# Two routing stages: x split in halves, the modulation behind the logits, fewer filler matmuls, an earlier table load

## The reference, cut to what matters

```python
for l in range(DEPTH):                       # DEPTH = 2
    mod = (silu(c) @ ada_w[l] + ada_b[l]).reshape(bsz, 6, 1, D_MODEL)
    sh1, sc1, g1, sh2, sc2, g2 = (mod[:, i] for i in range(6))
    h = rms_norm(x, norm1_g[l]) * (1.0 + sc1) + sh1
    x = x + g1 * mixer(h)                    # even layer: gating + differential attention; odd: dilated attention + conv
    h = rms_norm(x, norm2_g[l]) * (1.0 + sc2) + sh2
    x = x + g2 * grouped_moe(h, router_w, router_b, moe_w_gu[l], moe_w_down[l])

def grouped_moe(h, ...):
    probs = softmax(t @ router_w)            # 16 experts
    sel = (probs + router_b).reshape(-1, 4, 4)
    grp = argmax(sum of the top 2 of each group); experts = the top 2 in that group
    gates = p_top / sum(p_top)
    act = silu(g) * u * gate_dense           # g, u: h @ w_gu[e], 1024 x 1024 an expert
    y = einsum('etf,efd->td', act, w_down)   # 512 x 1024 an expert
```

## Time and profile before

| | |
|---|---|
| median of 3 runs | 871.66 us (870.56, 871.66, 875.34) |
| the profiled execution | 875.81 us |
| its span, first to last instruction | 874.0 us |
| PE / DVE / ACT / POOL busy | 90% / 43% / 20% / 2% of the span |
| PEld busy | 47% |
| mean granted clock of TensorE | 0.976 of 2.4 GHz |
| DMA | 294 MB, mean 336 GB/s |

### The profile page before, as it was taken

One profiled execution on the slowest core, in us unless ns is written; L12 is line 12 of the kernel. 1 busy time (PEld: TensorE's weight loads), 2 busy tenths in 40 slices (PEclk: granted clock), 3 DMA queues, 4 the chain that ended last, 5 costly groups with the idle time before them and its releaser, 6 DMA issues.

```text
span 874.0 us, 12136 instructions
## 1 busy us (share of the span) xinstructions
PE 789.9 (90%) x4984; PEld 412.6 (47%) x4984; DVE 375.0 (43%) x892; ACT 174.9 (20%) x413; POOL 14.5 (2%) x61
## 2 busy tenths in 40 slices
PE   4999999999999998778999999898999999898864
PEld 2566454454343333224858778764454333333221
DVE  1188862573322230205699765354563312221203
ACT  2041321511111110103000423451511111110101
POOL 2000010000000000000000000000000000000000
PEclk9999999999999999979999999999989999999978
DMA  9999998797899999999999225204977899999993
GB/s 348 389 386 387 387 387 322 298 374 277 328 427 425 426 424 427 427 421 390 385 386 357 97 97 193 98 1 145 428 272 285 333 430 423 428 423 428 427 421 150
DMA packets 65115, 294.05 MB, mean 336 GB/s; under 512 B 2721, under 2 KB 3361, under 8 KB 49185
## 3 DMA queue, kind: packets, MB, share of 16 engines
q1 hardware_dynamic: 64352, 290.62, 83.8%
q10 hardware_dynamic: 560, 2.10, 0.6%
q0 software_dynamic: 144, 0.52, 0.2%
HBM read 292.18 MB, written 1.05 MB: 336 GB/s over the span
## 4 chain that ended last, share of the span: by engine, by line
PE 52%; issue 24%; DMA 12%; DVE 6%; ACT 4%; POOL 0%; DVEq 0%; SPq 0%; POOLq 0%; ACTq 0%
PE bank L856 16%; PE bank L852 11%; PE bank L1103 8%; DMA ring<-w_gu_dram 7%; DMA ring<-w_down_dram 5%; PE bank L1125 4%; PE bank L1089 3%; PE bank L737 2%; PE bank L697 1%; PE bank L1140 1%; PE bank L761 1%; ACT tail L1314 1%; PE bank L752 1%; PE bank L714 1%; PE bank L923 1%
## 5 line engine op out<-in xcount | busy, mean ns | idle before, releaser
L1103 PE MATMUL bank<-ring,scr 128*64 128x512 f32 (+1 forms) x1024 | 197.0, 629 | 34.6 <-DMA ring<-w_gu_dram 22.2
L856 PE MATMUL bank<-hT,ring 128*128 128x256 f32 x640 | 142.3, 381 | 0.4 <-DVE hT L1668 0.4
L1103 PEld LDWEIGHTS bank<-ring,scr 128*64 128x64 f32 (+1 forms) x1024 | 56.3, 132 | 162.7 <-issue 131.8
L856 PEld LDWEIGHTS bank<-hT,ring 128*128 128x128 f32 x640 | 120.5, 190 | 17.8 <-issue 1.6
L1125 PE MATMUL bank<-ring,scr 128*64 128x512 f32 (+1 forms) x544 | 106.0, 625 | 5.4 <-DMA ring<-w_down_dram 5.0
L1598 DVE SCALAR_TENSOR_TENSOR gb<-ring,small,gb 128x512 f32<-128x512 f32 x84 | 63.1, 752 | 2.9
L1125 PEld LDWEIGHTS bank<-ring,scr 128*64 128x64 f32 (+1 forms) x544 | 30.6, 131 | 62.4 <-issue 60.5
L852 PE MATMUL bank<-ring,xh 128*128 128x512 f32 x128 | 56.9, 598 | 0.7 <-ACT xh L1314 0.7
L852 PE MATMUL bank<-ring,hT 128*128 128x512 f32 x128 | 56.4, 596 | 0.6 <-ACT hT L1348 0.5
L2105 DVE SCALAR_TENSOR_TENSOR hT<-bank,small,gb 128x512 f32<-128x512 f32 x26 | 19.5, 751 | 84.1 <-PE bank L1125 82.6
L1859 DVE SCALAR_TENSOR_TENSOR tail<-scr,col,tail 128x256 f32<-128x256 f32 x120 | 47.9, 474 | 0.0
(11 more groups left out here) (266 smaller groups left out, 761.3 us busy)
## 6 DMA issues: line engine op xcount, KB each, us to landing
ring<-w_gu_dram SPq DMA_DIRECT2D x60, 2048.0 KB, 20.4
ring<-w_down_dram SPq DMA_DIRECT2D x28, 2048.0 KB, 17.9
ring<-ada_w_dram SPq DMA_DIRECT2D x24, 2048.0 KB, 15.8
ring<-od_w_in_dram SPq DMA_DIRECT2D x9, 2048.0 KB, 19.9
ring<-ev_w_in_dram SPq DMA_DIRECT2D x5, 2048.0 KB, 19.7
ring<-w_down_dram SPq DMA_DIRECT2D x8, 1024.0 KB, 27.6
scr<-w_gu_dram SPq DMA_DIRECT2D x10, 512.0 KB, 7.9
ring<-ev_w_out_dram SPq DMA_DIRECT2D x2, 2048.0 KB, 17.9
```

What stands on the lines that cost most here:

```text
L856: ins = pe.matmul(banks[h][:, m * 256:(m + 1) * 256], w[:, c, (2 * h + m) * P:(2 * h + m + 1) * P], x_part[:, c, :], start=(c == 0 and m = ...
L1103: ins = pe.matmul(b[o:o + r, :].rearrange("p (u f) -> p u f", u=2), h[:, c, r * i:r * i + r], wm, start=(first and c == 0), stop=(last and ...
```

## The change

- `x_hi` and `x_lo` are made in halves of 512 columns, two for each tile. On ACT: half 0 of tile 0, the copy of the router's sums, half 1 of tile 0, then in `route` both halves of tile 1. On DVE: half 0 of tile 0 before the logits are read, half 0 of tile 1 before the slot map, the two halves 1 behind it. The first bank of gathers waits for the halves 0 alone.
- `mod_by_fours` writes to bank 5 instead of 6 and comes behind the logits' matmuls; its copy `modp` comes after the choice. ACT and DVE wait for it before they modulate gathered rows.
- The column sums are four matmuls of 128 columns each instead of sixteen of 32. In layer 0 the fourth sum comes behind the triangle matmuls.
- `keep_busy` in `route`: in layer 0 from 1 + 5 + 1 to none, in layer 1 from 1 + 7 to 3.
- The gates' four instructions on DVE move behind the slot map and the halves 1.
- The dummy `Exp` that fetches the table moves from `norm` into `even()`, behind the last Gelu.

```diff
@@ -308,11 +308,11 @@
-        def by_fours(a):
-            return a.rearrange("p (h q c) -> p h c q", h=2, c=4)
-        def by_chunks(a):
-            return a.rearrange("p (h c q) -> p h c q", h=2, c=4)
+        def fours(a):
+            return a.rearrange("p (q c) -> p c q", c=4)
+        def chunks4(a):
+            return a.rearrange("p (c q) -> p c q", c=4)
@@ -551,7 +551,7 @@
                     if (kind, k) == ("X", NATURAL):
-                        sp.wait_ge(lo_ready, 2 * (l + 1))
+                        sp.wait_ge(lo_ready, 4 * (l + 1))
                         sp.wait_ge(row_sum, 4 + 2 * l)
@@ -716,7 +716,6 @@
                 if ph % 2 == 1:
-                    mod_by_fours(ph)
                     pe.wait_ge(hT_dve, 4 * (ph + 1))
@@ -725,9 +724,10 @@
                 pe.wait_ge(x_ready, ph + 1)
+                pe.wait_ge(acc_out, 2 + 4 * l)
                 for a in range(4):
                     for c in range(4):
-                        ins = pe.matmul(bank[6][32 * a:32 * a + 32, 256 + c:272:4], ident[:, c::4],
+                        ins = pe.matmul(bank[5][32 * a:32 * a + 32, 256 + c:272:4], ident[:, c::4],
                                         mod[:, l, 24 + a:40:4], start=True, stop=True, skip_group_check=True)
@@ -782,7 +782,10 @@
                 pe.wait_ge(acc_out, n + 1)
-                ins = column_sums(bank[6], 4 * (n % 4), acc_experts[n % 4], thirty_second)
+                for m in range(4):
+                    ins = pe.matmul(bank[6][:, 4 * (n % 4) + m:4 * (n % 4) + m + 1],
+                                    acc_experts[n % 4][:, m * P:(m + 1) * P], thirty_second, start=True, stop=True,
+                                    skip_group_check=True)
                 ins.then_inc(row_sum, 1)
@@ -1048,7 +1051,6 @@
-                pe.wait_ge(modp_out, l + 1)
                 for c in range(KC):
@@ -1056,18 +1058,18 @@
                 pe.wait_ge(pick_step, 3)
-                keep_busy(1, bank[0])
                 pe.wait_ge(acc_out, 3)
                 give(misc, ins)
+                mod_by_fours(2 * l + 1)
                 if l == 0:
                     next_row(3)
-                for n in range(4 * l, 4 + 2 * l):
+                for n in range(4 * l, 3 + 3 * l):
                     next_row_sum(n)
-                keep_busy(5 + 2 * l, bank[0])
+                keep_busy(3 * l, bank[0])
                 pe.wait_ge(oh_ready, l + 1)
@@ -1076,7 +1078,7 @@
                 if l == 0:
-                    keep_busy(1, bank[0])
+                    next_row_sum(3)
                 else:
@@ -1226,8 +1228,8 @@
-                pe.wait_ge(lo_ready, 2 * (l + 1))
                 for g, n, k in FIRST_ROWS:
+                    pe.wait_ge(lo_ready, 4 * l + 2 * n + 2)
                     rows(g, n, k)
@@ -1331,8 +1333,9 @@
-            def high_part(t):
-                act.activation(by_chunks(x_hi[:, t, :]), by_fours(xh[:, t, :]), ACT.Copy).then_inc(hi_ready, 1)
+            def high_part(t, h):
+                act.activation(chunks4(x_hi[:, t, h * W:(h + 1) * W]), fours(xh[:, t, h * W:(h + 1) * W]), ACT.Copy)\
+                   .then_inc(hi_ready, 1)
@@ -1349,11 +1352,10 @@
                     act.wait_ge(xh_ready, 2 * ph + 2)
-                    high_part(0)
+                    high_part(0, 0)
                     act.wait_ge(router_part, l + 1)
                     act.activation(router_sum, bank[6][:, 0:2 * P], ACT.Copy).then_inc(router_out, 1)
-                    act.activation(sm(895, 1), ones[:, 0:1], ACT.Exp)
+                    high_part(0, 1)
@@ -1421,13 +1423,16 @@
+                def exp_table():
+                    act.activation(sm(895, 1), ones[:, 0:1], ACT.Exp)
                 def u_out(h):
                                  [lambda: late_row_out(11), gelu_table],
-                                 [lambda: u_out(0)], [lambda: u_out(1)]])
+                                 [lambda: u_out(0)], [lambda: u_out(1), exp_table]])
                 for c0 in (0, 4):
@@ -1485,10 +1490,12 @@
                 act.activation(pr, lg, ACT.Exp).then_inc(pr_ready, 1)
-                act.wait_ge(xh_dve, 4 * l + 4)
-                high_part(1)
                 if l == 0:
                     row_out(3)
+                act.wait_ge(xh_dve, 4 * l + 4)
+                for h in range(2):
+                    high_part(1, h)
+                act.wait_ge(modp_out, l + 1)
@@ -1669,11 +1676,11 @@
-            def low_part(l, t):
-                dve.wait_ge(hi_ready, 2 * l + t + 1)
-                dve.tensor_tensor(by_chunks(x_lo[:, t, :]), by_fours(xh[:, t, :]),
-                  by_chunks(x_hi[:, t, :].bitcast(F32)), ALU.subtract)\
-                   .then_inc(lo_ready, 1)
+            def low_part(l, t, h):
+                dve.wait_ge(hi_ready, 4 * l + 2 * t + h + 1)
+                o = slice(h * W, (h + 1) * W)
+                dve.tensor_tensor(chunks4(x_lo[:, t, o]), fours(xh[:, t, o]), chunks4(x_hi[:, t, o].bitcast(F32)),
+                                  ALU.subtract).then_inc(lo_ready, 1)
@@ -1683,9 +1690,7 @@
                 if s == 1:
-                    dve.wait_ge(modp_full, l + 1)
-                    dve.tensor_copy(modp[:, l, :], bank[6][:, 256:272]).then_inc(modp_out, 1)
-                    low_part(l, 0)
+                    low_part(l, 0, 0)
@@ -2002,20 +2007,23 @@
                 dve.wait_ge(oh_ready, l + 1)
+                dve.wait_ge(modp_full, l + 1)
+                dve.tensor_copy(modp[:, l, :], bank[5][:, 256:272]).then_inc(modp_out, 1)
+                if l == 1:
+                    dve.wait_ge(row_sum, 6)
+                    dve.tensor_tensor(mod[:, 1, 40:48], bank[6][:, 0:8], col[:, C_ADAB + 88:C_ADAB + 96], ALU.add)\
+                       .then_inc(rows_added, 1)
+                low_part(l, 1, 0)
+                misc_in()
+                step(dve.scalar_tensor_tensor(out=rg[:, 0:2, :], in0=bank[7][:, 0:32].rearrange("p (t e) -> p t e", t=2),
+                                              scalar=1.0, in1=oh1, op0=ALU.add, op1=ALU.mult))
+                slot_map(pcur[0], rg, 0)
+                for t in range(T):
+                    low_part(l, t, 1)
                 step(dve.tensor_tensor(gates, pr, oh1, ALU.mult))
                 step(dve.tensor_tensor(rg[:, 2:4, :], gates, one2[3].unsqueeze(2).to_broadcast([P, 2, 16]), ALU.mult))
-                if l == 1:
-                    dve.wait_ge(row_sum, 6)
-                    dve.tensor_tensor(mod[:, 1, 40:48], bank[6][:, 0:8], col[:, C_ADAB + 88:C_ADAB + 96], ALU.add)\
-                       .then_inc(rows_added, 1)
-                low_part(l, 1)
-                misc_in()
-                step(dve.scalar_tensor_tensor(out=rg[:, 0:2, :], in0=bank[7][:, 0:32].rearrange("p (t e) -> p t e", t=2),
-                                              scalar=1.0, in1=oh1, op0=ALU.add, op1=ALU.mult))
-                slot_map(pcur[0], rg, 0)
                 dve.tensor_copy(rg[:, 5, :], bank[7][:, 32:48]).then_inc(misc_free, 1)
@@ -2126,6 +2134,7 @@
+                dve.wait_ge(modp_out, l + 1)
                 rows(0, 1, 3)
                 capacity(l)
```

## The result

The change makes the kernel slower: 880.88 us, the median of 4 executions (880.78 to 881.72), against 871.11 us of the kernel before run beside it (4 executions, 869.81 to 875.34). The ratio is 1.0096, interval 1.0065 to 1.0126. Forecast were 870.5 us, a range of 866.5 to 874.2, and "no change" with a chance of 0.70. All of that missed. The four executions of before lie low: in the larger samples that stand beside the experiments (17 to 30 executions) its median is 872.80 to 873.23 us, and against the 872.80 a second set of the changed kernel (e5) is 7.6 us slower, not 9.8.

What follows compares the result with a forecast made beforehand. Transfers pace the expert bodies, but PE's routing sets when they begin. Layer 0 +0.1 and layer 1 -1.6 gave -1.5 us, less 0.4 for an unlucky profile: 871.66 - 1.1 = 870.5 us, range 866.5 to 874.2.

Steps and rivals of the forecast that it cites:

- the shift goes through one for one: Expert bodies: transfers set the pace, but a routing stage that ends earlier moves everything behind it by the same amount.
- the 1.7 us forecast: Layer 0, up to the choice: earlier logits and a halved `x_lo` let DVE start the choice 1.7 us earlier.
- The gathers of layer 0: Layer 0, slots to `up(0, 1)`: 32 gathers at the slow clock, 0.213 us each, 6.8 us.
- The table load: Load and dummy in `even()`, 1.48 us, ahead of a copy with 1.00 us idle time: +0.48 us.
- The wide sums, hidden by PE's gaps (exposed, at most 0.5 us): Both routings: wide column sums count as nothing, covered by PE's idle time; at most 0.5 us if exposed.
- some 0.4: Layer 0, PE behind the logits: twelve wide sums priced at some 0.4 us, off the path.
- The second term: PE ahead of the triangle: products 1.92 us, layer 1's three fillers about 0.9 each; slow clock expected in the gathers.
- the 2.6 us of gap: Layer 0, PE before the choice: about 2.6 us idle, cover for modulation, products and sums, nothing on the path.
- until 631.5: Layer 1, PE behind the logits: modulation 1.44, sums 0.3 and three fillers end at 631.5 us, hidden before the choice.
- The baseline: Profiled execution, 4.15 us above the 871.66 median, perhaps unlucky for the clock; 0.4 us taken off, leaving a 1.1 gain.
- The clock stays low through all of `up(0, 0)`: Rival, both layers: `up(0, 0)` takes 7.2 us; +2.7 and +1.0, together +3.7, 875.4 us; chance 12%.
- That of DVE's wait: Rival, clock stays high: fast gathers, `up(0, 1)` waits for DVE in both layers; -5.8, 865.8 us; chance 20%.
- The gain does not get through: Rival, expert bodies: first experts start earlier but transfers end as before; 871.7 to 872.2 us; chance 13%.

Runs made afterwards that it cites:

- e2: The changed kernel with the table load back behind the router's copy and tile 0's second x_hi half behind the Exp; 879.68 us, ratio 1.0077.
- e12: The kernel of e9 with the table load back behind the router's copy and tile 0's half 1 of x_hi behind the Exp; 871.64 us, ratio 0.9980.
- e7: The kernel before with only its fillers cut as in the change: none in layer 0, three in layer 1; 878.72 us, ratio 1.0062.
- e8: The changed kernel with narrow sums, some fillers back in both layers, and DVE's rows(0, 1, 3) ahead of the second slot map; 872.69 us, ratio 0.9999.
- e11: The kernel of e6 with the modulation by fours back ahead of the router, in bank 6; 875.63 us, ratio 1.0025.
- e4: The kernel before with only the table load moved into the mixer; 872.41 us, ratio 0.9992.
- e10: The kernel before with only the modulation by fours moved behind the logits, in bank 5, its copy behind the choice; 870.35 us, ratio 0.9966.
- e9: The kernel of e6 with DVE reordered: tile 0's second x_lo half ahead of the triangle's copy, rows(0, 1, 3) ahead of the second slot map; 871.86 us, ratio 0.9984.
- e6: The changed kernel with narrow column sums and all of before's fillers back; 877.79 us, ratio 1.0055.
- e1: The changed kernel with the column sums narrow again, 16 matmuls of 32 columns each; 875.54 us, ratio 1.0038.

## Why the prediction was wrong

**What held.** PE, DVE and the expert bodies were read rightly: the shift goes through one for one (432.44 us in both). The choice ended 12.0 us after the entry, against 13.4 before: 1.4 of the 1.7 us forecast. The gathers of layer 0 ran slow, 7.0 us for 6.8 forecast, and `up(0, 0)` took 5.15 for 4.65 (3.6 + 1.05). The table load took 0.4 us in its row, for 0.48.

**The failed step** is "The wide sums, hidden by PE's gaps (exposed, at most 0.5 us)", with the "some 0.4" for twelve of them and 0.3 for eight. I took four matmuls in place of sixteen to be cheaper. The twelve measured 2.84 us, the eight of layer 1 3.57 at the low clock, the four behind the triangle 1.84. In layer 1 that is 3.3 us more than forecast, ahead of the triangle, and past the cover; in layer 0 the train ends 0.6 us past the choice, and the fourth sum holds the gathers 0.5 us. What sets the price is the weight load, which has 128 columns for one column of output:

```profile
174.78 2.75 PEld L786 LDWEIGHTS bank<-small,gb 128*128 128x128 f32 x24 [1.32 <-issue]
```

That is 0.115 us a load, in a train without gaps; the narrow ones, of 32 columns in four groups, stood 0.011 us apart (96 in 1.04 us). The Trainium skill (TensorE: Matmul & The Clock Gate, "LDWEIGHTS (loading the stationary operand)") says that a load takes its number of columns divided by 1.2, in ns. The 24 loads at full clock agree with it: by it they would be 2.56 us, an estimate from that page, for 2.75 measured. It names no other price at the low clock, and there the measurement decides: 23 loads took 4.98 us in e2, twice as much. I had weighed a rule on the table load and not this one.

**The second term** is the clock ahead of the triangle. In layer 0 the row of products was priced at 1.92 us and took 3.5, which used up 1.6 of the 2.6 us of gap that were to cover everything; the five triangle matmuls took 2.05 us (177.49 to 179.54) for 1.2. I gave layer 1's three fillers 0.9 us each; they took 5.47 together. In layer 1 I put the slow clock into the gathers; it fell on sums and fillers instead, ahead of the triangle, 5.9 us later than "until 631.5" in all (641.15 less the shift of 3.77 is 637.4), and 3.6 of it past the choice.

**The baseline.** I took the profile before as an unlucky one and subtracted 1.1 us from the median of 871.66, as if the change met the same luck. It doesn't. Executions of before range from 869.5 to 878.5 us: beside e12 the ones at 870.2 had a mean clock of 0.985, those at 875.2 to 875.6 one of 0.974 or 0.975. The changed kernel never went under 878.9 in 10 executions, with clocks of 0.962 to 0.964. By these clocks before pays for slow stretches in some executions only, the changed kernel in all; the profile of before is one of its longer executions (875.81 us), so the profiles lie 4.97 us apart where the medians lie 7.6 to 9.8. e7 shows the price of the missing fillers alone, some 6 us: 12.0 us of work run where 7.2 did. The forecast counted the slow gathers, but against a baseline that had part of such losses already.

What lets the clock fall stays open. In e7 PE idles ahead of the gathers; in the changed kernel it doesn't idle from 169.77 us on (the gaps ahead are 1.30 and 0.59 us), and the clock falls all the same, at 171 and again near 178. What the two share is that the fillers are gone.

**The entry** was 1.46 us late, not 0.48. The slow stretch at 123 us stands in four of the eight profiles with the early table load (both of the changed kernel, e8, e11) and in none of the six without; e4, which has the load, doesn't show it and loses nothing. A link is likely; eight profiles don't prove it. The Trainium skill (TensorE: Matmul & The Clock Gate, Part 1) says that slow stretches of one kernel vary by run, and the two profiles of the changed kernel agree: `up(0, 1)` of layer 1 took 3.65 us in one and 5.35 in the other.

**The rivals.** "The clock stays low through all of `up(0, 0)`" named a rise later than 4 us in layer 0; 5.15 us for a 3.6 leave 1.55, so it came about 3.1 us into it (3.4 by the clock of 0.78 from 191 to 192 us), and that rival did not happen, though its 875.4 us was the nearest of the forecast's numbers. That of DVE's wait happened in layer 1 (2.14 us), where I had it only with a fast clock in both layers. "The gain does not get through" is answered by the 432.44 us, and by e4 and e10, where an earlier `up(0, 1)` went through. No rival joined a mis-sized edit with lost cover, though "exposed, at most 0.5 us" rested on no row.

## What to carry to other kernels

Price a matmul by the columns of its weights too, not by how many instructions there are: one matmul with 128 weight columns and one output column took 0.118 us recorded, eleven times a 32-column one in four groups. Fillers ahead of a critical burst are worth their time when without them the burst takes twice as long (7.0 us instead of 3.7 in layer 0); that other work fills their place on PE, as in the changed kernel, is no proof that they can go. Try the cut by itself first, as e7 does. And when a burst gets faster, look at once for what the other engine has queued behind the step that released it (here two halves and the gates, 2.9 us): mended in that order, the parts of this change go from 1% slower to the level of before or just under it (e9, e12), and its cheapest part alone (e10) to 0.34% faster.

## What the runs showed of the hardware

- The weight-load-bound train of wide matmuls ran twice as slow at the low clock (24 records in 5.28 us in e2, 2.84 at full clock; its loads at 0.217 us each, 23 in 4.98, against 0.115), so its loads go with TensorE's clock.
- TensorE fell to 1.2 GHz and stayed there while it was busy without a gap: 13.00 of 13 us from 178 to 191 us, with triangle matmuls, the fourth sum, gathers of 128 columns and `up`. No gap stood in that stretch, nor from 171 to 174 us, where the clock was 0.50 too.
- A wait of 2.37 us on an otherwise full-clock path (e6) was followed by half clock at 190.5 us, and the next 16 matmuls took 5.35 us instead of 3.60, another 1.75 us. So it went in e11 (2.38 us, then 5.35) and in layer 1 of e5 (2.13, then 5.35); but waits of 2.13 to 2.18 us at the same place in layer 1 of the changed kernel, e1, e2, e6 and e11 were followed by 3.65 us, at full clock. What decides between the two, no run shows.
